# Query and key projections with 512-column products over the high and low parts of x

## The reference, cut to what matters

```python
proj = hn @ w_in                       # hn = rmsnorm(x), 256 x 1024
qkv, z, b, a = jnp.split(proj, [...], axis=-1)
qkv = jax.nn.silu(causal_dwconv(qkv, conv_w))
q, k, v = jnp.split(qkv, [GDN_QK_DIM, 2 * GDN_QK_DIM], axis=-1)
q = l2norm(q.reshape(bsz, t, 8, 128)) * (128 ** -0.5)
k = l2norm(k.reshape(bsz, t, 8, 128))
```

## Time and profile before

| | us |
|---|---|
| median of 3 runs (1174.56 to 1175.34) | 1174.6 |
| the profiled execution's own time | 1175.85 |
| its span, first to last instruction | 1173.8 |
| PE busy | 1158.7 (99%) |
| POOL busy | 871.7 (74%) |
| ACT busy | 736.7 (63%) |
| DVE busy | 613.0 (52%) |

### The profile page before, as it was taken

The page is one execution under the profiler, slowest core; times in us unless marked ns, Lnnn a source line. Parts: engine busy times, 40 slices in busy tenths (PEclk is TensorE's granted clock), DMA queues, the critical chain, the costliest instruction groups (busy, mean ns, idle before and its releaser), DMA issues.

```text
span 1173.8 us, 21474 instructions
## 1 busy us (share of the span) xinstructions
PE 1158.7 (99%) x7040; PEld 1003.1 (85%) x7040; DVE 613.0 (52%) x1643; ACT 736.7 (63%) x1442; POOL 871.7 (74%) x373
## 2 busy tenths in 40 slices
PE   8999999999999999999999999999999999999997
PEld 7998899888888889878888888888798888888886
DVE  5667767536655465457655555291362426323234
ACT  6777677656766667756766666664375546655553
POOL 5846744377988887637988889878778466988883
PEclk9999999999999999999999999999999999999999
DMA  7678522256765555515655554656456343665550
GB/s 284 200 148 206 175 89 91 72 180 198 249 194 195 185 187 187 177 58 163 216 192 197 181 194 164 197 197 203 156 169 226 108 151 119 220 196 193 188 170 36
DMA packets 61352, 202.85 MB, mean 173 GB/s; under 512 B 6480, under 2 KB 13008, under 8 KB 61152
## 3 DMA queue, kind: packets, MB, share of 16 engines
q1 hardware_dynamic: 53712, 193.51, 50.3%
q10 hardware_dynamic: 7568, 8.39, 3.8%
HBM read 197.68 MB, written 4.19 MB: 172 GB/s over the span
## 4 chain that ended last, share of the span: by engine, by line
PE 95%; DVE 3%; ACT 1%; issue 1%; DMA 0%; SPq 0%; DVEq 0%; ACTq 0%
PE bank L183 18%; PE bank L185 17%; PE bank L184 17%; PE solve L198 10%; PE bank L198 9%; PE solve L208 5%; PE bank L208 5%; PE bank L995 1%; PE solve L1009 1%; PE bank L1581 1%; PE bank L192 1%; PE bank L1604 1%; DMA raw<-in_stream 0%; PE solve L1590 0%; PE bank L1888 0%
## 5 line engine op out<-in xcount | busy, mean ns | idle before, releaser
L167 POOL TENSOR_TENSOR wlo<-raw,whi 128x1024 fp32r<-128x1024 f32 x362 | 862.8, 2412 | 272.4 <-ACT whi L163 272.3
L163 ACT ACTIVATE whi<-raw 128x1024 fp32r<-128x1024 f32 x362 | 380.5, 1057 | 125.9 <-PE bank L185 123.3
L183 PE MATMUL bank<-whi,xpair 128*128 128x512 f32 (+2 forms) x456 | 178.4, 391 | 0.1
L185 PE MATMUL bank<-whi,xpair 128*128 128x512 f32 (+2 forms) x456 | 173.9, 381 | 0.0
L184 PE MATMUL bank<-wlo,xpair 128*128 128x512 f32 (+2 forms) x456 | 173.8, 381 | 0.0
L198 PE MATMUL solve<-xpair,whi 128*128 128x512 f32 x528 | 137.3, 392 | 0.2
L198 PE MATMUL bank<-xpair,whi 128*128 128x512 f32 x480 | 124.6, 391 | 0.0
L183 PE MATMUL bank<-xpair,whi 128*128 128x256 f32 (+1 forms) x408 | 120.0, 294 | 1.8 <-DVE xpair L2505 1.2
L184 PE MATMUL bank<-xpair,whi 128*128 128x256 f32 (+1 forms) x408 | 115.2, 282 | 0.0
L185 PE MATMUL bank<-xpair,wlo 128*128 128x256 f32 (+1 forms) x408 | 115.1, 282 | 0.0
L198 PEld LDWEIGHTS solve<-xpair,whi 128*128 128x128 f32 x528 | 96.9, 189 | 18.3 <-issue 1.1
(11 more groups left out here) (456 smaller groups left out, 1870.6 us busy)
## 6 DMA issues: line engine op xcount, KB each, us to landing
raw<-in_stream SPq DMA_DIRECT2D x363, 512.0 KB, 3.5
band_scratch<-band ACTq DMA_DIRECT2D x1, 3072.0 KB, 36.2
area<-band_scratch ACTq DMA_DIRECT2D x2, 1024.0 KB, 10.4
scr<-in_row_b_gate ACTq DMA_DIRECT2D x1, 1024.0 KB, 4.7
out<-resid SPq DMA_DIRECT2D x4, 256.0 KB, 2.0
tab<-in_tabs SPq DMA_DIRECT2D x1, 640.0 KB, 9.6
resid<-in_x SPq DMA_DIRECT2D x1, 512.0 KB, 3.7
resid<-in_x SPq DMA_DIRECT2D x2, 256.0 KB, 5.1
```

The source lines that it names most:

```text
L163: act.activation(whi[:, n.s, :], raw[:, n.s, :], ACT.Copy).then_inc(hi_ready, 1)
L167: pool.tensor_tensor(wlo[:, n.s, :], raw[:, n.s, :], whi[:, n.s, :].bitcast(F32), ALU.subtract).then_inc(lo_ready, 1)
L183: nc.tensor.matmul(out_ap, a_hi, b_hi, start=start, stop=False)
L185: return nc.tensor.matmul(out_ap, a_lo, b_hi, start=False, stop=stop)
```

## The change

The units of blocks 1 to 15 run through `pairs_still` in place of `weights_still` (block 0 keeps its form, and so do the value units). For these blocks ScalarE copies columns 256 to 511 out of the bank to `qk_low` (`low_rows`), and VectorE adds the copy to the first half, waits for that, and multiplies by the root as before. `conv_scaled(b)` now waits for the copy (`CV.low`) and not for the unit. The order on ScalarE becomes `low_rows(b)`, `conv_finish(b - 1)`, `refill`, `conv_first(b)`, `sum_squares(b - 3)`. One semaphore of the start (`rel_row`) is folded into another (`warm`).

```diff
+        qk_low, _ = carve(16 * SEQ, 2, SEQ)
@@ qk_pe
-                    weights_still(pe, unit(BASE["qk"] + b), [proj_bank(b)[:, 0:SEQ]], KD, 0)
+                    pairs_still(pe, unit(BASE["qk"] + b), proj_bank(b))
@@ conv_scaled
-            dve.wait_ge(unit_done, (BASE["qk"] + b if b < 16 else BASE["v"] + b - 16) + 1)
             bank = proj_bank(b)[:, 0:SEQ]
+            if 0 < b < 16:
+                dve.wait_ge(CV.low, b)
+                dve_link(dve.tensor_tensor(bank, bank, qk_low[:, b % 2, :], ALU.add))
+            else:
+                dve.wait_ge(unit_done, (BASE["qk"] + b if b < 16 else BASE["v"] + b - 16) + 1)
             dve.tensor_tensor(bank, bank, rbc[:], ALU.mult).then_inc(CV.scaled, 1)
@@
+        def low_rows(act, b):
+            act.wait_ge(unit_done, BASE["qk"] + b + 1)
+            if b >= 3:
+                act.wait_ge(CV.scaled, b - 1)
+            act.activation(qk_low[:, b % 2, :], proj_bank(b)[:, SEQ:2 * SEQ], ACT.Copy).then_inc(CV.low, 1)
@@ qk_act
             for b in range(16):
-                conv_first(act, b)
                 if b == 0:
+                    conv_first(act, b)
                     round_unit(act, unit(5))
                     refill(act, BASE["ba"])
                     masks(act)
-                if b >= 1:
+                else:
+                    low_rows(act, b)
                     conv_finish(act, b - 1)
                 refill(act, BASE["qk"] + b)
+                if b:
+                    conv_first(act, b)
                 if b >= 3:
                     sum_squares(act, b - 3)
```

More of the change, by code:

```diff
@@ L710, in ffn_dve @@
             low_part(NF - 1, 0)
-        CV = sems("conv", "root bcast root_copied scaled first conv silu square turned copied_k")
+        CV = sems("conv", "low root bcast root_copied scaled first conv silu square turned copied_k")
         GT = sems("gate", "copied ba rates absx logs g cum cum_copied masks")
@@ L850, in qk_pe @@
                     pe.wait_ge(IN.rel, 16)
-                    pe.wait_ge(IN.rel_row, 1)
+                    pe.wait_ge(IN.warm, 3)
                     pe.matmul(ps[7][0:16, 128:128 + BANDX], rel[0:33, :], tabv("buckets")[0:33, 0:BANDX], start=True,
@@ L2414, in block2_dve @@
                                          ALU.mult, ALU.add).then_inc(rescaled, 1)
-        IN = sems("in", "tabs ident a_norm cols small pos rel x0 x1 x1_rest band_ps band band_out sin warm rel_row angle")
+        IN = sems("in", "tabs ident a_norm cols small pos rel x0 x1 x1_rest band_ps band band_out sin warm angle")
         rel = sb("rel", [P, 16])
@@ L2494, in start_dve @@
             dve.memset(root_tmp[:], 0.0).then_inc(IN.warm, 1)
-            dve.memset(rel[32:33, :], -BIG).then_inc(IN.rel_row, 1)
+            dve.memset(rel[32:33, :], -BIG).then_inc(IN.warm, 1)
             dve.wait_ge(hi_ready, 1)
```

## The result

| | us |
|---|---|
| kernel before, median of 5 runs (1174.56 to 1175.34; the 3 known ahead are among them) | 1174.82 |
| changed kernel, median of 5 runs (1184.69 to 1187.07) | 1186.01 |
| ratio | 1.0093, 95% interval 1.0082 to 1.0104 |
| difference | +11.2 |
| the changed kernel's profiled execution: time, span | 1185.57, 1183.5 |

The account below looks back on a forecast made before the run. It took the loop of ACT and DVE, 3.33 us a turn and 3.53 in blocks 6 to 12, as the stage's bound. The shift of 8.7 plus 0.3 gave 1174.6 + 9.0 = 1183.6 us, 8 in 10 from 1179.3 to 1187.3.

Parts of the forecast that it names:

- The loop closed by the order: On ACT and DVE, silu, rounding, `conv_first` and taps follow one another: 3.33 us a turn against PE's 3.03.
- Where PE closes it further: Blocks 6 to 12: PE's unit waits for DVE's key copy and ACT's low copy for the unit, 3.53 us a turn.
- path of 7.07 for two turns: Blocks 6 to 12: key copy, transposes, unit, low copy, silu, rounding, `conv_first` and taps sum to 7.07 us.
- The add and the multiply lie beside silu and rounding: DVE's add and multiply run beside ACT's silu and rounding and cost nothing; without that cover, 0.9 us.
- the gates' turn: Block 3: the gates' operations hold DVE 0.96 us ahead of the add, so the turn is 3.84 us.
- The columns' gain of 1.0: PE's 15 units: 24 narrow products become 16, saving 0.06 to 0.07 us each, 1.0 in all if nothing waits.
- the weight loads as bound: Rival: PE waits for weight loads; 120 fewer in the 15 units give -14.4 us, 1160.2; 3%.
- The start: `conv_scaled(1)` waits for `low_rows(1)` behind ACT's four roundings and two masks; PE stands some 3 us at block 1's transposes.
- the table load: ACT's activation table load at the start, 1.28 us, taken as hidden before silu(0); bounds 0 and 1.28.
- The sign that was set for PE's waits ahead of 75 us: The forecast is wrong if PE's waits before 75 us sum to much less than 9.
- a rival of 15%: PE's clock falls in its new waits; unit 6 at half speed takes 2.9 us more, 1186.5 us; 15%.
- The collision of the earlier trace: DVE's L978 took 1.77 us beside GpSimd's operation; taken as 0.2 after, up to 1.4 more if it collides again.

Follow-up runs that it names:

- The order alone: Kernel before with silu and rounding put ahead of `conv_first` on ScalarE; no copy, no add, no paired products: 1182.75 us, +7.2, ratio 1.0063.
- the order one block ahead: Changed kernel with ScalarE's copy of b + 1 ahead of `conv_first(b)`, VectorE's add of b + 2 behind multiply b + 1, transposes one unit later: 1175.92 us, +0.8.
- the clock kept up: Changed kernel with three products of 384 columns into an overwritten bank in each of TensorE's two long waits: 1184.38 us, +8.8, ratio 1.0079.
- the start put right: Changed kernel with block 1's low copy right behind `conv_first(0)` and block 0's taps ahead of block 1's add: 1186.2 us, +11.1, ratio 1.0098.
- the end moved: Kernel one block ahead, with block 13's transposes behind the z unit's halves and the last rounding behind silu(15): 1176.23 us, +1.2, ratio 1.0011.

## Why the prediction was right, and where it was off

**The loop closed by the order: right, shown.** Turns of 3.31 for 3.33, of 3.83 for 3.84. The order alone makes it, an instruction in it lengthens it and one beside it doesn't, and the order one block ahead, with the transposes one unit later, removes it with all the added work in place.

**"Where PE closes it further": right, in the rows.** Blocks 6 to 12 take 24.04 us with the order alone and 25.70 in the changed kernel with the clock kept up, 1.7 more with the low copy waiting for the unit; the forecast had 25.4 where seven turns of 3.33 are 23.3. The average of 3.53 hides where it begins: by the prediction's own path of 7.07 for two turns, block 6, behind a turn of 3.33, takes 3.74, and it took 3.83.

**"The add and the multiply lie beside silu and rounding": right, shown** by the kernel without the add, and by DVE's rows. The exception is the gates' turn, as forecast. That they cost 0.9 without that cover was seen too, where rounding went behind `conv_first`: 0.46 and 0.47 of that turn are theirs.

**The columns' gain of 1.0: half of it, 0.5,** with zero inside the interval; the weight loads as bound are refuted. The page Perfetto Trace Analysis of the Trainium skill, section Identifying the Most-Contended Engine, takes the busy share of the weight loads as a measure of how near TensorE is to its limit. That fewer loads give back time was the prediction's own step from it, and here they didn't, though loads were busy 91% of the stage.

**The start: the rows right, the reading too simple.** The transposes of block 1 started at 28.80 after a wait of 2.87, "some 3 us"; the table load ran from 22.66 to 23.94, ahead of silu(0) at 25.02, and cost nothing, as taken. But the start put right gave nothing, since ACT's own queue reaches silu(0) no sooner: the wait for the unit, three roundings (the text ahead says four; ACT's rows have three), two masks, the table load. The sign that was set for PE's waits ahead of 75 us, not "much less than 9", came out at 7.4; part of what they lack is in PE's slow matmuls, below.

**Blocks 6 to 12: 27.06 us, forecast 25.4. The mis-sized term is the clock's.** The sum took PE at full clock and left its fall to a rival of 15%. It fell. PE's rows of unit 6 in the changed kernel:

```profile
39.08 0.66 PE L810 MATMUL bank<-tab,area 128*128 128x128 f32 x2 [2.73 <-DVE area L986]
39.40 2.99 PE L198 MATMUL bank<-xpair,whi 128*128 128x512 f32 x7
42.23 1.11 PE L208 MATMUL bank<-xpair,wlo 128*128 128x256 f32 x8
```

Seven wide products take 2.99 where they take 1.77 in the earlier trace rows. The rival priced it at +2.9, half speed for the whole unit; by the windows half speed lasted until 41.9, so that only 2.8 us of the unit ran at it and 1.4 were lost. The turn came to 5.10, and with products in the waits it is 3.83. The price itself was read from the earlier trace rows, where the windows give 1.00 as granted clock; that those products ran slow shows only by their length, 0.70 a pass, against 0.35 a pass for products of the same form in the kernel with the clock kept up. The page TensorE: Matmul & The Clock Gate of the Trainium skill, section Why this matters for your kernels, had warned of it, and the windows agree: the clock is at 1.00 up to each of the two waits and at 0.50 when PE works again. Without the fall, blocks 2 to 15 take 49.5 us (28.32 to 77.84) where the forecast's recurrence has 49.3 (29.43 to 78.7).

**The sum.** Forecast 9.0; 1.3 to 2.4 for the clock and 0.2 for the turns give 10.5 to 11.6, against 11.2 measured. What else may be in it is within the intervals. By the traces, counted from `conv_first(0)` to the end of the taps of block 15, the loss of 10.8 is made of 4.0 at the start, 3.4 for the turns as the order alone has them, 0.5 for the add and multiply in the gates' turn, 1.7 for PE's unit in blocks 6 to 12 and 1.4 for the clock, less 0.1 in the other turns. The collision of the earlier trace rows did not happen in the changed kernel (0.17), as taken, but narrowly: GpSimd's subtraction ended at 65.91, 0.12 after the start of VectorE's operation at 65.79. It did happen where rounding went behind `conv_first` (1.47).

## What to carry to other kernels

When an operation is moved on an engine that works in order, write down who waits for whom from one block's step to the same step of the next, and compare the length of that loop with the bounding engine's turn; sums of busy time show nothing of it, and the same work in another order, with the transposes one unit later, was worth 10 us here. Put a dependent operation a full block behind its producer, and look for the second loop, which takes over when the first is opened. A stall of TensorE of some 3 us is to be priced with the clock that it loses, not only with its own length.

## What the runs showed of the hardware

**The clock.** In the changed kernel it fell to the lower of its two levels, 1.2 GHz, towards the end of the waits of 2.87 and 2.73 us, and stayed there for 2.8 us of work each time. With rounding behind `conv_first` it fell 0.4 us after a wait of 2.31 had ended. With only the order changed, two waits of 2.0 us came out differently: 1.4 us after the first had ended (at 28.36) the clock fell, with PE busy, and behind the second (at 38.26) it stayed at 1.00:

```profile
30.00:31.00 1.00, 1.00 (x7) 1.00 (x6) 0.93 (x3) 0.00 (x0) 1.00 (x2) 0.50 0.91 319
...
39.00:40.00 1.00, 1.00 (x11) 1.00 (x10) 0.29 (x1) 0.97 (x5) 0.60 (x1) 1.00 0.41 123
```

**VectorE and GpSimd.** The VectorE operation at the end of `key_roots`, 32 columns read from `gsc` and written to it, takes 0.18 us alone; where GpSimd's subtraction was running it ended when that ended. DVE and POOL with the end moved:

```profile
72.50 0.89 DVE L961 TENSOR_SCALAR gsc<-gsc 128x32 f32<-128x32 f32 x1
```
```profile
71.00 2.35 POOL L167 TENSOR_TENSOR wlo<-raw,whi 128x1024 fp32r<-128x1024 f32 x1 [1.82 <-ACT whi L163]
```

In the changed kernel the same operation (L958) takes 0.18. The one of the earlier trace rows, of the same form, took 1.77, and 1.47 to 1.78 in five others; in the changed kernel and six others it took 0.17. At the stage's start another (L2514 before, L2528 after, `col` to `col`) took 1.98 and 1.10, each to the end of a GpSimd subtraction; that is 0.9 of the 1.1 us by which the changed kernel's execution was ahead. Not every small operation is held. Just ahead of L978 in the kernel before, L975 and L976 (57.17 and 57.38, 32 columns too, but read from `solve`, which lies in PSUM) took 0.18 and 0.19 while the same subtraction ran. The Trainium skill, page SBUF — State Buffer, section SBUF: two separate sides, says that a VectorE operation in a two-port mode or with two inputs in SBUF and one of GpSimd take a shared pair of ports in turn, and that the one which starts first keeps it to its end. The lengths and ends above agree with that.
